# Reordering the small steps of a delta-rule mixer on one Trainium2 core: z ahead of the row picking, one picking product for both directions, a convolution and a z in halves

## The reference, cut to what matters

```
u = rms_norm(h, norm_mix_pre)                   # h: 272 x 1024
proj = u @ w_in                                 # q, k, v, z (512 each), gates, attention q, k, v
qkv = short_conv_silu(concat(q, k, v), conv_w)  # 5 taps over the tokens
q, k, v = split into 4 heads of 128; q and k l2-normalised
# per chunk of 64 tokens, per head, forward and backward in time:
a_low = where(strict, k k^T * decay * beta, 0)
u, w  = solve (I + a_low) x = rhs               # unit lower triangular
# then a scan over the chunks with the state S (128 x 128)
o = rms_norm(o_f + o_b, o_norm_w) * silu(z)
```

## Time and profile before

| | us |
|---|---|
| three runs | 1099.48, 1099.98, 1102.02 |
| median | 1099.98 |
| the profiled execution | 1098.76 |
| its span, first to last instruction | 1096.7 |
| PE busy in it | 1049.6 (96%) |
| DVE busy, ACT busy | 637.4, 563.3 |
| mean granted clock of TensorE | 0.991 |

### The profile page before, as it was taken

How to read it: one execution, slowest core, us unless ns; L and a number is a source line. 1 busy time by engine, 2 the same in 40 slices (tenths; PEclk the granted TensorE clock), 3 DMA queues, 4 the chain that set the end, 5 groups by cost and what they waited for, 6 DMA issues and landing times.

```text
span 1096.7 us, 17670 instructions
## 1 busy us (share of the span) xinstructions
PE 1049.6 (96%) x7381; PEld 954.9 (87%) x7381; DVE 637.4 (58%) x984; ACT 563.3 (51%) x1009; POOL 85.2 (8%) x84
## 2 busy tenths in 40 slices
PE   6999989999999999999899999999999999999997
PEld 5989877879999987988789999997999879999996
DVE  4687653586546457677866535448344466454554
ACT  5653354376444355556464434437676656343442
POOL 3012002010000001000100000000322210000000
PEclk9999999999999999999999999999999999999999
DMA  8322210055555546433346456464433334645641
GB/s 262 116 78 78 77 40 19 21 177 168 199 187 181 203 163 202 154 116 116 115 135 231 152 194 208 144 225 135 154 115 116 115 95 157 229 167 179 223 144 57
DMA packets 114974, 160.34 MB, mean 146 GB/s; under 512 B 3776, under 2 KB 99264, under 8 KB 114896
## 3 DMA queue, kind: packets, MB, share of 16 engines
q1 hardware_dynamic: 114896, 159.22, 43.7%
HBM read 158.16 MB, written 1.05 MB: 145 GB/s over the span
## 4 chain that ended last, share of the span: by engine, by line
PE 82%; DVE 9%; ACT 4%; issue 2%; POOL 1%; DMA 0%; SPq 0%; DVEq 0%; POOLq 0%; ACTq 0%
PE PS L652 23%; PE PS L654 22%; PE PS L653 22%; ACT SCR L1382 3%; DVE WL L1828 2%; PE PS L972 1%; PE PS L1343 1%; POOL SM L2412 1%; PE PS L686 1%; DVE SPARE L1828 1%; PE PS L1366 1%; PE PS L1264 1%; PE PS L967 1%; PE PS L1354 1%; DVE H L1864 1%
## 5 line engine op out<-in xcount | busy, mean ns | idle before, releaser
L1828 DVE TENSOR_TENSOR WL<-RAW,WH 128x1024 fp32r<-128x1024 f32 (+1 forms) x177 | 214.0, 1234 | 71.1 <-ACT WH L1382 70.8
L1382 ACT ACTIVATE WH<-RAW 128x1024 fp32r<-128x1024 f32 (+1 forms) x191 | 195.1, 1049 | 46.3 <-DMA RAW<-in_gu 28.5
L652 PE MATMUL PS<-UH,WH 128*128 128x256 f32 (+2 forms) x680 | 195.6, 288 | 5.0 <-DVE WL L1828 3.0
L654 PE MATMUL PS<-UH,WL 128*128 128x256 f32 (+2 forms) x680 | 194.6, 286 | 0.0
L653 PE MATMUL PS<-UL,WH 128*128 128x256 f32 (+2 forms) x680 | 194.5, 286 | 0.0
L1382 ACT ACTIVATE SCR<-PS 128x512 f32<-128x512 f32 (+7 forms) x233 | 100.7, 468 | 169.6 <-PE PS L654 118.2
L652 PEld LDWEIGHTS PS<-UH,WH 128*128 128x128 f32 (+1 forms) x680 | 130.0, 191 | 7.3 <-DVE WL L1828 3.5
L1828 DVE TENSOR_TENSOR SPARE<-RAW,SPARE 128x1024 fp32r<-128x1024 f32 x100 | 118.0, 1219 | 24.8 <-ACT SPARE L1382 24.8
L653 PEld LDWEIGHTS PS<-UL,WH 128*128 128x128 f32 (+1 forms) x680 | 129.5, 190 | 1.1
L654 PEld LDWEIGHTS PS<-UH,WL 128*128 128x128 f32 (+1 forms) x680 | 130.0, 191 | 0.5
L1382 ACT ACTIVATE SPARE<-RAW 128x1024 fp32r<-128x1024 f32 x100 | 100.3, 1047 | 29.8 <-DMA RAW<-in_gu 23.2
(11 more groups left out here) (307 smaller groups left out, 2094.4 us busy)
## 6 DMA issues: line engine op xcount, KB each, us to landing
RAW<-in_gu SPq DMA_DIRECT2D x44, 1024.0 KB, 5.3
RAW<-in_dn SPq DMA_DIRECT2D x22, 1024.0 KB, 7.3
RAW<-in_w_up SPq DMA_DIRECT2D x16, 1024.0 KB, 5.9
RAW<-in_w_down SPq DMA_DIRECT2D x16, 1024.0 KB, 4.9
RAW<-in_a_qkv SPq DMA_DIRECT2D x12, 1024.0 KB, 5.2
RAW<-in_w_in SPq DMA_DIRECT2D x11, 1024.0 KB, 5.3
RAW<-in_kv_w SPq DMA_DIRECT2D x8, 1024.0 KB, 6.1
RAW<-in_w_out SPq DMA_DIRECT2D x4, 1024.0 KB, 4.8
```

What stands on the lines that cost most here:

```text
L652: e.matmul(o, lh, rh, start=start, stop=False)
L654: return e.matmul(o, ll, rh, start=False, stop=stop)
L1382: return e.activation(o, i, func, bias=bias, scale=scale, accum_out=acc)
L1828: e.tensor_tensor(lo_of(n_), half_src(n_), hi_of(n_).bitcast(F32), SUB).then_inc(s_lo_dve, 1)
```

## The change

In `STAGE_1`: z.0 and low.13 go ahead of solve; the first half of conv.11 (`head.11`, four of its eight k) goes behind vtok.1 and ahead of in.1, the second half of it stands where conv.11 stood, now with meta.6 behind it; and the first half of z.3 (`head.3`) goes between qp.0 and gqa.1. z.0 to z.3 now write the banks 0, 1, 0 and 2. The picking in solve is done with one product for both directions for each s, with at most 168 columns, three s in bank 6 and four in bank 7, so DVE's operands of solve lie in one bank each. No edit touches the steps qp.2 or rows.0, in which norms of q are summed; qp.2 only stands behind head.3 now. The diff:

```diff
--- before.py
+++ after.py
@@ -65,10 +65,10 @@
 
 STAGE_1 = steps_of(
     "ba gates.0 conv.0 conv.1 taps.1 gates.1 conv.2 gates.2 conv.3 taps.3 gates.3 silu.0 kv.0 kv.1 ktok.0 ktok.1 kv.2 kv.3 "
-    "start.0 start.1 meta.0 low.10 q.0 q.1 inv.0 low.11 q.2 inv.1 meta.1 low.12 q.3 q.4 solve z.0 low.13 z.1 conv.4 inv.2 inv.3 "
+    "start.0 start.1 meta.0 low.10 q.0 q.1 inv.0 low.11 q.2 inv.1 meta.1 low.12 q.3 q.4 z.0 low.13 solve z.1 conv.4 inv.2 inv.3 "
     "meta.2 low.16 conv.5 rows.0 inv.4 inv.5 inv.6 meta.3 taps.5 inv.7 conv.6 low.17 inv.8 conv.7 low.18 rows.1 inv.9 meta.4 "
     "taps.7 inv.10 silu.1 rows.2 inv.11 conv.8 rows.3 low.20 inv.12 vtok.2 meta.5 conv.9 vtok.0 in.0 taps.9 rows.4 inv.13 low.21 "
-    "conv.10 vtok.1 in.1 meta.6 low.22 conv.11 inv.14 taps.11 silu.2 z.2 gqa.0 qp.0 gqa.1 qp.1 qp.2 gqa.2 z.3 gqa.3")
+    "conv.10 vtok.1 head.11 in.1 low.22 conv.11 meta.6 inv.14 taps.11 silu.2 z.2 gqa.0 qp.0 head.3 gqa.1 qp.1 qp.2 gqa.2 z.3 gqa.3")
 STAGE_2 = steps_of(
     " ".join(f"scan.0.{i} gqa.{2 * i + 4} scan.1.{i} gqa.{2 * i + 5}" + f" low.{22 + i}" * (0 < i < 4) for i in range(8)
              ).replace("gqa.19", "gt") +
@@ -492,7 +492,7 @@
         kv_a = marks("s_kv", *[(x, c) for c in range(3) for x in "xs"])
         q_a = marks("s_q", *[(x, c) for c in range(2) for x in "xs"])
         z_a = marks("s_z", 0, 1, ("x", 2), ("x", 3), 2, 3)
-        z_bank = (4, 5, 1, 3)
+        z_bank = (0, 1, 0, 2)
         kt_p = marks("s_ktok_pe", 0, 1, 2)
         kt_a = marks("s_ktok", *[x for c in range(3) for x in (*[("s", c, h) for h in range(4)], c)])
         kt_v = marks("s_ktok_dve", "e0", "e1", "rk2", "b0", "b1")
@@ -516,7 +516,8 @@
         me_v = marks("s_meta_dve", ("m", 0), ("m", 1), "m80", "nc0", "m81", "nc1", "e0", "e1", "a", "b", ("u", 0), ("u", 1))
         me_o = marks("s_meta_pool", "m", ("k", 0), ("k", 1))
         compact = lambda t: t.rearrange("p (d m j) -> p d m j", d=2, m=12)
-        SLOT = [12 * sum(7 - i for i in range(s)) for s in range(8)]
+
+        picked = [24 * sum(7 - i for i in range(3 * (s > 2), s)) for s in range(7)]
 
         CORNER = ((slice(0, 64), slice(64, 128)), (slice(64, 128), slice(0, 64)))
         qp_p = marks("s_qk_pe", 0, 1, "n")
@@ -738,17 +739,19 @@
                                 ins.then_inc(*first_p.step((r, 0)))
                 return first
 
-            def up(n, bank, o0, o1, uh, ul, ready):
+            def up(n, bank, o0, o1, uh, ul, ready, ks=range(8)):
 
                 wh, wl = both(n)
                 pe.wait_ge(*LO[n])
-                pe.wait_ge(*emptied[bank])
+                if 0 in ks:
+                    pe.wait_ge(*emptied[bank])
                 rows = wh.shape[2]
-                for k in range(8):
+                for k in ks:
                     pe.wait_ge(*ready[k])
                     ins = mm3(PS[0:rows, bank, o0:o0 + uh.shape[2] - o1], wh[:, k, :], wl[:, k, :], uh[:, k, o1:], ul[:, k, o1:],
                               k == 0, k == 7)
-                ins.then_inc(s_half, 1)
+                if 7 in ks:
+                    ins.then_inc(s_half, 1)
 
             def token_half(n, banks, k0, uh, ul, off, ready):
 
@@ -878,8 +881,15 @@
                         ins.then_inc(*gt_p.step(j))
                         emptied[j] = gt_a[j]
 
+            def head(i):
+
+                if i == 11:
+                    up(HALF_CONV[i], conv_bank(i), 0, 0, UH, UL, u0, range(4))
+                else:
+                    up(half_of(("z", i // 2), i % 2), z_bank[i], 0, 16, UH, UL, u0, range(4))
+
             def conv(i):
-                up(HALF_CONV[i], conv_bank(i), 0, 0, UH, UL, u0)
+                up(HALF_CONV[i], conv_bank(i), 0, 0, UH, UL, u0, range(4, 8) if i == 11 else range(8))
                 emptied[conv_bank(i)] = cv_v[i, 4]
 
             def kv(c):
@@ -907,7 +917,7 @@
                     emptied[4], emptied[5] = q_a["s", 0], q_a["s", 1]
 
             def z(h):
-                up(half_of(("z", h // 2), h % 2), z_bank[h], 0, 16, UH, UL, u0)
+                up(half_of(("z", h // 2), h % 2), z_bank[h], 0, 16, UH, UL, u0, range(4, 8) if h == 3 else range(8))
                 emptied[z_bank[h]] = z_a[h if h < 2 else ("x", h)]
 
             def turn_rows(c, b0, b, done):
@@ -1006,12 +1016,13 @@
                     pe.wait_ge(*m["nc"])
                 pe.wait_ge(*me_v["nc1"])
                 pe.wait_ge(*solve_o["nc0"])
-                for d in range(2):
-                    pe.wait_ge(*emptied[6 + d])
-                    for s in range(7):
-                        ins = e.matmul(PS[:, 6 + d, SLOT[s]:SLOT[s + 1]], SEL[:, 128 * s:128 * s + 128], compact(NC)[:, d, :, s + 1:],
-                                       start=True, stop=True)
-                    emptied[6 + d] = solve_v["t", 6]
+                rows = NC.rearrange("p (m j) -> p m j", j=8)
+                for s in range(7):
+                    b = 6 + (s > 2)
+                    pe.wait_ge(*emptied[b])
+                    ins = e.matmul(PS[:, b, picked[s]:picked[s] + 24 * (7 - s)], SEL[:, 128 * s:128 * s + 128], rows[:, :, s + 1:],
+                                   start=True, stop=True)
+                emptied[6], emptied[7] = solve_v["t", 2], solve_v["t", 6]
                 ins.then_inc(solve_p, 1)
 
             def meta(i):
@@ -1221,7 +1232,7 @@
             def og(k):
                 out_half(1, half_of(("out", 1, k // 2), k % 2), k, mix_ready(1, k), k == 4)
 
-            in_order(STAGE_1, dict(gqa=gqa, ba=ba, gates=gates, conv=conv, kv=kv, q=q, z=z, ktok=ktok, vtok=vtok, start=start, inv=inv, meta=meta,
+            in_order(STAGE_1, dict(gqa=gqa, ba=ba, gates=gates, conv=conv, head=head, kv=kv, q=q, z=z, ktok=ktok, vtok=vtok, start=start, inv=inv, meta=meta,
                                solve=solve, qp=qp, **{"in": gqa_in}))
             in_order(STAGE_2, dict(scan=scan, gqa=gqa, gt=gqa_turn, on=on, og=og))
             out_last(1, [half_of(("out", 1, k // 2), k % 2) for k in range(4)], range(4), [mix_ready(1, k) for k in range(4)])
@@ -2074,14 +2085,14 @@
 
             def solve():
 
-                n, x, t = (y.rearrange("p (d m j) -> p d m j", d=2, m=12) for y in (NC, XC, TC))
+                x, t = (y.rearrange("p (m j) -> p m j", m=24) for y in (XC, TC))
                 dv.wait_ge(solve_p, 1)
                 for s in range(7):
                     dv.wait_ge(*(solve_v["x", s - 1] if s else solve_o["xc0"]))
-                    rows = PS[:, 6:8, SLOT[s]:SLOT[s + 1]].rearrange("p d (m j) -> p d m j", m=12)
-                    e.tensor_tensor(t[:, :, :, 0:7 - s], rows, bc(x[:, :, :, s], 7 - s, 3), MUL).then_inc(*solve_v.step(("t", s)))
+                    rows = PS[:, 6 + (s > 2), picked[s]:picked[s] + 24 * (7 - s)].rearrange("p (m j) -> p m j", m=24)
+                    e.tensor_tensor(t[:, :, 0:7 - s], rows, bc(x[:, :, s], 7 - s, 2), MUL).then_inc(*solve_v.step(("t", s)))
                     dv.wait_ge(*solve_v["t", s])
-                    e.tensor_tensor(x[:, :, :, s + 1:], x[:, :, :, s + 1:], t[:, :, :, 0:7 - s], SUB).then_inc(*solve_v.step(("x", s)))
+                    e.tensor_tensor(x[:, :, s + 1:], x[:, :, s + 1:], t[:, :, 0:7 - s], SUB).then_inc(*solve_v.step(("x", s)))
 
             def meta(i):
                 v = PS[0:16, 6, 0:128].rearrange("p (a b) -> p a b", a=8)
```

## The result

| | executions | median, us | ratio to before (95% interval) |
|---|---|---|---|
| before | 5 | 1101.76 | |
| changed | 5 | 1089.52 (1088.47 to 1094.96) | 0.9908 (0.9888 to 0.9929) |
| before, beside the last four kernels | 11 | 1101.38 | |
| changed, the same kernel again | 5 | 1090.08 (1088.68 to 1091.22) | 0.9900 (0.9884 to 0.9916) |

The account below looks back on a forecast made before the run. PE was taken to bound the kernel (82% of the chain, no transfer in it); 5.2 + 1.3 + 0.8 + 0.5 = 7.8 us won gave a median of 1092.2 us, range 1089.1 (both late clock falls gone) to 1096.

Parts of the forecast that it names:

- likeliest case: The forecast itself: at least part of a clock fall saved, gains over 7.2 us, 1089.5 to 1092.8 us; chance 0.52.
- z ahead of solve and one picking product: Around solve: 5.2 us won, 2.4 of waiting, 1.7 of picks, 1.1 of half clock.
- Bank 0 for z.2: At z.2: no more wait for ACT to free bank 1, 1.3 us won (bounds 0 and 1.3).
- conv.11 in halves: Around in.1 and meta.6: full passes between narrow work save half the clock fall, 0.8 us (1.6 won to 1.7 lost).
- The fall behind meta.5: Half clock at 132.0 to 135.5 us; its steps are unchanged, so it was left as it is.
- head.3: At qp.2: z.3 passes fill its 1.32 us wait, 0.9 returns at gqa.3's transposes, 0.5 us won.
- signs of being wrong: inv.3 waiting for DVE or ACT's silu, 0.50 clock covering z.1, or gqa.3 to span end over 1 us longer.
- C: Behind the mixer: a wait hanging on a transfer grows by as much; gain under 2.2 us, 1098 to 1100; chance 0.05.
- Rival A: Late part: the clock falls as often as before; gain 7.0 us, time 1093.0; chance 0.25.
- B: At solve: picks cost by columns, 3.5 us not 1.8, z.2 may still wait; 1096.0 to 1094.7 us; chance 0.15.
- D: At inv.3: held for bank 1 by z.1's late silu, slower, 1103.5 us if freed at 90; chance 0.03.
- E's reading: The change speaks of an order of q norms, but no diff line changes one; worth nothing in any case.

Follow-up runs that it names:

- E1: Kernel before plus only z.0 and low.13 ahead of solve, z.0 and z.1 in banks 0 and 1, one picking product: 1094.56 us, 0.9945 of before.
- E6: Changed kernel with each picking product made twice (28 passes, 1344 columns): 1092.35 us, executed once for its profile.
- E9: Kernel before plus ten unused identity products ahead of the wait of solve: 1097.94 us, 0.9973 of before.
- E7: Kernel before with only the one picking product for both directions: 1098.77 us, 0.9981 of before.
- E2: Changed kernel with solve, its picks and the banks of z.0 and z.1 as before, so the late part alone: 1096.68 us, 0.9957 of before.
- E5: Changed kernel with z.0 to z.3 in the old banks 4, 5, 1 and 3: 1092.55 us.
- E3: Changed kernel with conv.11 whole behind meta.6, as before: 1090.65 us, 0.9909 of before.
- E4: Changed kernel with z.3 whole between gqa.2 and gqa.3: 1093.24 us, 0.9928 of before.
- E8: Changed kernel with conv.9 in halves too, its first half ahead of meta.5: 1088.66 us, 0.9891 of before.
- E11: Changed kernel with conv.9 in halves and three unused products ahead of in.0: 1089.29 us, 0.9897 of before.
- E12: Changed kernel run again, unaltered: 1090.08 us, 0.9900 of before.

## Why the prediction was right, and which term was too small

The forecast was 1092.2 us; measured were 1089.52 and 1090.08. Both lie in the range from 1089.1 to 1096, near its fast end, which I had worked out with both late falls of the clock gone; 1089.52 lies at the very edge of the likeliest case's own range (1089.5 to 1092.8). The direction and the steps around solve were forecast. That the number fell within the range owes something to its width. By its own steps:

- z ahead of solve and one picking product, 5.2 us: E1 gave 5.5, with noise of about 2 us. z.0 starts at 68.97, right behind q.3; the picks took 1.57 us (1.8 forecast), inv.3 came at 79.33 (79.5). DVE's low parts ended in time, solve's pairs ran from 73.55, inv.2 from 77.72 (77.7). The count of passes decides, shown by E6.
- But inside this term the clock was mis-sized. I counted 1.1 us for it, from one execution in which it was low for 3.4 us behind solve. Even that fall cost more: with the wait filled, inv.3 came 1.7 us sooner in E9's profile. E7's profile has 6.8 us at the low level there and E2's 10.2, and E9 is 3.1 us faster than before by the means.
- Bank 0 for z.2, 1.3 us: no wait there now. In E5 the old bank costs z.2 only 0.89 us, and 2.2 us together with z.0's.
- conv.11 in halves, 0.8 us: E3 gives 1.0 by the means, not told apart from nothing. My premise was that narrow work pulls the clock down, not waiting alone; at solve the runs show that it is the waiting (E9, and E7, where the clock fell ahead of the first pick). In the profiled execution the clock stayed at 1.00 from 139.5 to 149.3 and fell in z.2 instead, to which meta.6 and inv.14 are the work before. The fall behind meta.5, which I had left as it was, took 6.8 us there instead of 3.4.
- head.3, 0.5 us from waits: the new wait at gqa.3 is 0.80 us (0.9 forecast), qp.2 waits for nothing. Whether it has a worth in clock, for which I had put nothing, stays open: E4 points to it, the other profiles don't bear it out.
- The sum: 7.8 us, of which 5.9 from waits and passes and 1.9 from the clock. Measured 10.4 by the means, of which 4.8 to 7.0 from waits and passes (5.4 in the pair of profiles) and 3.4 to 5.7 from the clock. The term that was too small is the clock's: forecast was a third to a little over half of what was measured. I had sized it from the one execution whose trace I had.
- One of my signs of being wrong came true: the time from gqa.3 to the end of the span was 928.3 us and is 929.9, 1.6 longer, which was to be C. It isn't C. Against E5's profile, which has the same work there and no fall, PE is busy 1.6 us longer and idle just as long: that is the fall of the clock at 487 us, not a wait that grew. Where the clock doesn't fall around 500, the changed order takes as long to the end as before does (E5, E8 and E11 in the table above).
- Rival A (the clock falls as often as before in the late part) isn't refuted. The mean clock is that of the whole span, and the fall behind solve alone can account for much of its rise; in the late part the two profiles of the changed kernel have 10.2 and 3.4 us at the low level, that of before 6.8. B is refuted by E6, C and D by the time; E's reading stands: no order of norms changed.
- The Trainium skill's rule (TensorE: Matmul & The Clock Gate, section Part 1: The HAM clock gate), that an idle array falls back to the low clock, fares better than I let it. Where PE's standing still ahead of the picks was filled (E9: 0.9927 against 0.9903) the clock came back, and where only narrow work was cut (E7: 0.9907) it did not. Yet in the profile of the changed kernel the clock also falls behind meta.6 and inv.14, with PE busy 3.17 of 3.20 us, so standing still is not the whole of it.

What stays open: which of the late steps brings the clock down in a given execution. The profiles have it low at different places of the same work: the same meta.6 and inv.14 that stand ahead of the fall at 149.3 us in the changed kernel are followed by none in E5, E8, E11 and E12. And eleven of the fourteen have a fall between 484 and 532 us, between 745 and 761, or both, in work that no experiment touched. Only a record of where the clock falls in many executions would settle it.

## What to carry to other kernels

Where PE, busy till then, waits for a microsecond or two, the wait can cost more than its length, because the clock may fall behind it: the wait of 2.3 us came with a fall in each of its three profiles; E5 (waits up to 1.27 us) and E11 (up to 0.9) have no fall in the mixer. Price it by several executions' mean clocks, not by one profile. A block of full products that has its weights and a free bank is the best thing to move there, cut in halves where one gap is too short for it; and its bank must be one that was left long ago, or the wait only changes its name. Small products cost by their number: one with twice the columns, up to 168 here, is nearly free.

## What the runs showed of the hardware that I had not expected

The low level comes and goes between executions of one program: of 45 executions of the kernel before, the mean clock was 0.985 to 0.993, and their times 1098.4 to 1104.9 us. In E5's profile the clock was at the low level only near the two ends of the span (mean 0.998), while E4's had it low three times between 125 and 166 us. And a fall at one place can be two or three times as long: behind the wait of solve it was 3.4 us in one profile, 6.8 and 10.2 in two others. What a fall costs hangs on its place: about 1.6 us for 3.4 at the low level around 500 us of the span, and 0.3 at most around 750.
